# The last expert's rows reach the tokens by one-hot products, all other rows are gathered earlier; index keys loaded in pieces; a shorter routing

## What is computed

```python
def hier_moe(h, w_group, b_group, w_router, b_router, w_gate, w_up, w_down):
    ...
    g_w, g_idx = lax.top_k(jax.nn.softmax(g_logits, axis=-1), 1)
    ...
    e_in = e_logits[jnp.arange(m), g_idx[:, 0]]
    top_v, top_i = lax.top_k(e_in, TOP_K_INNER)
    top_w = jax.nn.softmax(top_v, axis=-1) * g_w
    ...
    for e in range(N_EXPERTS):
        hid = jax.nn.silu(x2 @ w_gate[e]) * (x2 @ w_up[e])
        y = y + combine[:, e:e + 1] * (hid @ w_down[e]).astype(jnp.float32)
```

## Time and profile before

| | |
|---|---|
| median of 3 runs | 1548.93 us (1548.56 to 1549.74) |
| profiled execution, its own time | 1553.47 us |
| its span | 1551.6 us |
| PE, DVE, ACT, POOL busy | 1360.3, 606.3, 305.6, 124.9 us |
| granted PE clock, mean | 0.928 |
| DMA | 341.04 MB, mean 220 GB/s |

### The profile page before, as it was taken

The page is one execution under the profiler, slowest core; times in us unless marked ns, Lnnn a source line. Parts: engine busy times, 40 slices in busy tenths (PEclk is TensorE's granted clock), DMA queues, the critical chain, the costliest instruction groups (busy, mean ns, idle before and its releaser), DMA issues.

```text
span 1551.6 us, 28263 instructions
## 1 busy us (share of the span) xinstructions
PE 1360.3 (88%) x10889; PEld 765.2 (49%) x10890; DVE 606.3 (39%) x1542; ACT 305.6 (20%) x777; POOL 124.9 (8%) x374
## 2 busy tenths in 40 slices
PE   7999998899689999998599987888999599998990
PEld 4454454454555555554543433455646365555550
DVE  2169733251513111110547997666303422111115
ACT  2121133321100000001303112455601000000102
POOL 1010190001000000000200000000000100000002
PEclk9999989899789999999599998899999699999995
DMA  8523567761658999998301021332443479999975
GB/s 266 200 52 119 187 200 229 226 264 41 249 196 323 360 391 398 399 402 341 128 5 55 31 109 55 110 108 73 131 175 120 156 304 344 394 387 388 396 289 194
DMA packets 87385, 341.04 MB, mean 220 GB/s; under 512 B 25671, under 2 KB 32935, under 8 KB 73286
## 3 DMA queue, kind: packets, MB, share of 16 engines
q1 hardware_dynamic: 67246, 289.40, 50.8%
q0 software_dynamic: 10656, 37.56, 7.1%
q10 hardware_dynamic: 9344, 12.20, 2.3%
HBM read 309.00 MB, written 30.47 MB: 219 GB/s over the span
## 4 chain that ended last, share of the span: by engine, by line
PE 63%; DVE 14%; DMA 12%; SPq 4%; issue 4%; ACT 2%; POOL 1%; POOLq 0%; ACTq 0%; DVEq 0%
PE banks L1161 19%; DMA arena<-in_wstream 9%; PE banks L840 9%; PE banks L1189 8%; PE banks L1067 6%; DVE arena L1746 4%; PE banks L868 3%; SPq L458 2%; PE banks L818 2%; PE banks L987 2%; DVE arena L1874 2%; DVE arena L1868 2%; PE banks L798 1%; DVE arena L1896 1%; DVE arena L1893 1%
## 5 line engine op out<-in xcount | busy, mean ns | idle before, releaser
L1161 PE MATMUL banks<-arena 128*32 128x128 f32 (+1 forms) x4736 | 363.3, 337 | 25.5 <-DMA arena<-in_wstream 13.1
L1161 PEld LDWEIGHTS banks<-arena 128*32 128x32 f32 (+1 forms) x4736 | 242.7, 127 | 145.3 <-issue 52.7
L1189 PE MATMUL banks<-arena 128*64 128x512 f32 (+1 forms) x1184 | 173.3, 492 | 1.1 <-ACT arena L1641 1.1
L1746 DVE TENSOR_TENSOR arena<-arena,banks 128x256 f32<-128x256 f32 (+5 forms) x84 | 38.5, 459 | 278.5 <-PE banks L1161 181.2
L840 PE MATMUL banks<-arena 128*128 128x512 f32 x320 | 144.0, 605 | 0.5 <-DMA arena<-in_wstream 0.5
L2118 DVE COPY arena<-banks 128x256 f32<-128x256 f32 (+1 forms) x56 | 21.4, 382 | 295.6 <-PE banks L1174 289.3
L1746 DVE TENSOR_TENSOR arena<-banks,arena 128x512 f32<-128x512 f32 (+5 forms) x159 | 70.7, 474 | 137.0 <-ACT arena L1565 81.3
L1067 PE MATMUL banks<-arena 128*128 128x512 f32 x256 | 115.4, 609 | 3.6 <-ACT arena L1681 2.3
L868 PE MATMUL banks<-arena 128*128 128x512 f32 x256 | 118.1, 606 | 0.0
L1641 ACT ACTIVATE arena<-banks 128x512 f32<-128x512 f32 (+1 forms) x56 | 29.6, 529 | 369.3 <-PE banks L1189 369.3
L1189 PEld LDWEIGHTS banks<-arena 128*64 128x64 f32 (+1 forms) x1184 | 59.6, 123 | 83.7 <-issue 68.3
(11 more groups left out here) (278 smaller groups left out, 1419.0 us busy)
## 6 DMA issues: line engine op xcount, KB each, us to landing
arena<-in_wstream SPq DMA_DIRECT2D x109, 2048.0 KB, 13.2
arena<-in_fox_kt SPq DMA_DIRECT2D x64, 256.0 KB, 3.1
arena<-in_fox_v SPq DMA_DIRECT2D x64, 256.0 KB, 3.0
arena<-in_dsa_page SPq DMA_DIRECT2D x64, 256.0 KB, 3.1
expert_rows<-arena ACTq DMA_DIRECT2D x76, 128.0 KB, 9.1
expert_rows<-arena POOLq DMA_DIRECT2D x1, 6656.0 KB, 19.4
hn_scratch<-arena POOLq DMA_DIRECT2D x8, 512.0 KB, 2.9
expert_rows<-arena ACTq DMA_DIRECT2D x68, 32.0 KB, 8.2
```

What stands on the lines that cost most here:

```text
L1161: last = mm(bank(b, 0, 4 * n, n * j, n * j + n), x[:, c, :], w[:, c, 4 * n * j:4 * n * j + 4 * n], start=(c == 0), stop=(c == DC - 1))
L1189: last = mm(bank(3, 0, 8 * n, n * q, n * q + n), ht2[g % 2][:, 128 * i + n * j:128 * i + n * j + n], w[:, c, 8 * n * q:8 * n * q + 8 * n], ...
L1746: return v.tensor_tensor(out, x, y, op)
```

## The change

Three edits. **(1)** The down product of the last group of slot 14 (g = 25) moves ahead of the up product of g = 26. POOL waits only for the stores of groups 0 to 25 and issues the ten gathers of the combine then (`combine` before `spilled`); a token whose row belongs to the last expert reads a row of zeros (ZROW, 128 rows more are zeroed at the start). The two groups of the last expert are not stored: they stay in SBUF (`y2`, `y_last`), and PE makes for each tile a product of a one-hot matrix `match` (which token each row belongs to, built by DVE at g = 10 and 11) with them (`last_expert`). DVE adds first all ten gathered pieces (`landed_rows`), then for each tile the product with the weight `w_last` (`combine_tile`). The row arithmetic of DVE is spread over g = 7 to 11. **(2)** The 64 key loads are cut into pieces of 12, 12, 26, 8 and 6 between the weight blocks. **(3)** In `route`, two steps become one, one loses its wait, a pair of memsets becomes one earlier memset, and a subtraction moves behind `mask`.

```diff
+SAVED = ENDS[NE - 2]
+ZROW = NROWS + SPILLS * CAP
...
-        for s in range(NS):
-            for j in range(NPG):
+
+        def index_keys(n0, n1):
+            for n in range(n0, n1):
+                s, j = divmod(n, NPG)
...
             if l == 0:
+                index_keys(0, 12)
                 sp.wait_ge(S("ln_done"), 1)
                 first_weights(0, 1, 0)
+                index_keys(12, 24)
             sp.wait_ge(S(f"out_mm{l}"), upto(f"out_mm{l}", 5))
             first_weights(l, 0, 1)
+            if l == 0:
+                index_keys(24, 50)
             sp.wait_ge(S(f"out_mm{l}"), upto(f"out_mm{l}", 10))
             first_weights(l, 0, 2)
+            if l == 0:
+                index_keys(50, 58)
             sp.wait_ge(S(f"route_mm{l}"), upto(f"route_mm{l}", 1))
             first_weights(l, 1, 2)
+            if l == 0:
+                index_keys(58, NS * NPG)
...
         def combine(l):
 
-            pool.wait_ge(S(f"row_u{l}"), upto(f"row_u{l}", 1))
+            pool.wait_ge(S(f"row_u{l}"), upto(f"row_u{l}", 2))
+            pool.wait_ge(S("zeros_out"), 16)
+            pool.wait_ge(S(f"xg_used{l}"), upto(f"xg_used{l}", NE))
+            pool.wait_ge(S(f"up_mm{l}"), upto(f"up_mm{l}", SAVED))
             for i in range(4):
-                pool.wait_ge(S(f"y_rows{l}_{i}"), upto(f"y_rows{l}_{i}", max(STORED[i::4])))
+                pool.wait_ge(S(f"y_rows{l}_{i}"), upto(f"y_rows{l}_{i}", max(STORED[i:SAVED:4])))
             for t in range(NT):
                 for k in range(2):
                     i = 2 * t + k
+                    if i == 7:
+                        pool.wait_ge(S(f"gate_mm{l}"), upto(f"gate_mm{l}", GROUPS))
...
+                if g == SAVED:
+                    down(g - 1)
...
-                if g > 0:
+                if g == GROUPS - 1:
+                    down(g - 1, lambda: turn_hid(g))
+                elif g > 0 and g != SAVED:
                     down(g - 1)
-            turn_hid(GROUPS - 1)
             down(GROUPS - 1)
+
+        def last_expert(l):
+
+            def share(t, i, y, n):
+                b = (4, 6, 0, 2, 0)[t]
+                for k in range(2):
+                    last = mm(bank(b + k, 0, 512, 0, rows(t)), match[i][64 * k:64 * k + n, 128 * t:128 * t + rows(t)],
+                              y[64 * k:64 * k + n, :], start=(i == 0), stop=(i == 1))
+                if i == 1:
+                    last.then_inc(S(f"down_mm{l}"), 1)
...
+            for t in range(2, NT):
+                if t == 4:
+                    pe.wait_ge(S(f"combined{l}"), upto(f"combined{l}", 3))
+                share(t, 0, y2[(GROUPS - 2) % 4], 64)
+                share(t, 1, y_last, 32)
...
+            v.memset(ghot[64:128, 4, :], 0.0).then_inc(S("dve_chain"), 1)
+            dve.wait_ge(S("dve_chain"), chained())
...
-            v.tensor_scalar(g3(sm[6], NT), hots[0], NEG, None, ALU.mult).then_inc(S("dve_chain"), 1)
+            v.scalar_tensor_tensor(out=e_in, in0=hots[0], scalar=NEG, in1=e_in, op0=ALU.mult, op1=ALU.add)\
+                .then_inc(S("dve_chain"), 1)
             dve.wait_ge(S("dve_chain"), chained())
-            tt(e_in, e_in, g3(sm[6], NT), ALU.add).then_inc(S("dve_chain"), 1)
-            dve.wait_ge(S("dve_chain"), chained())
...
+        def landed_rows(l):
+
+            for t in range(NT):
+                if t > 0:
+                    dve.wait_ge(S(f"yb{l}_{t}"), upto(f"yb{l}_{t}", 32))
+                for k in range(2):
...
+                    step(weighted(t, k))
...
         def combine(l):
             n = 2 * l + 2
-            for t in range(NT + 2):
+            dve.wait_ge(S(f"turns{l}"), upto(f"turns{l}", 1))
+            flag = spill_flag(dve)
+            landed_rows(l)
+            spilled(l, flag)
+            for t in range(NT + 3):
                 if t < NT:
                     combine_tile(l, t)
                 if 1 <= t <= NT:
                     mean_square(n, t - 1)
-                if t >= 2 and l == 0:
-                    to_xt(n, t - 2)
+                if t >= 3 and l == 0:
+                    to_xt(n, t - 3)
```

More of the change, by code:

```diff
@@ L396, in further_rounds @@
                         body(i)
+            if at_end:
+                at_end()
     def page_rows(ap, page):
@@ L1176, in turn_hid, with down @@
                 last.then_inc(S(f"ht_mm{l}"), 1)
-            def down(g):
+            def down(g, between=None):
                 s, off, n = PARTS[g]
@@ new lines, in _, with late_rows @@
+        row_of, over = g3(rtmp[0], NT), g3(rtmp[3], NT)
+        def late_rows(l):
+            some = g3(rtmp[1], NT)
+            step(tt(over, pos, bc_mid(cap_e, NT), ALU.is_ge))
+            step(tt(row_of, over, bc_mid(delta, NT), ALU.mult))
+            step(tt(row_of, row_of, pos, ALU.add))
+            step(v.scalar_tensor_tensor(out=row_of, in0=row_of, scalar=-float(ZROW), in1=bc_mid(base_e, NT),
+                                        op0=ALU.add, op1=ALU.add))
+            step(tt(some, row_of, over, ALU.mult))
+            per_choice(some, sm[3], float(ZROW))
+            v.tensor_copy(row_late, sm[3][:, 0:2 * NT])
@@ L2097, in xgt_evac, with last_matches @@
+        def last_matches(l):
+            for i in range(2):
+                for t in range(NT):
+                    last = v.tensor_scalar(match[i][:, 128 * t:128 * t + rows(t)], slot16[:, 0:rows(t)], 128.0 * t,
+                                           slot_tok[i], ALU.add, ALU.is_equal)
+            last.then_inc(S(f"row_u{l}"), 1)
         def xgt_evac(l, par, banks, n, done):
@@ L2155, in turn, with late_rows @@
                 tt(hid, g3(sil, 4), g3(bank(1), 4), ALU.mult).then_inc(S(f"general{l}_"), 1)
-            dve.wait_ge(S(f"turns{l}"), upto(f"turns{l}", 1))
-            further_rounds(dve, turn)
+            def late_rows():
+                dve.wait_ge(S(f"late{l}_"), 16 * 2 * NT)
+                for k in range(2):
+                    for t in range(NT):
+                        last = weighted(t, k)
+                    last.then_inc(S(f"late_sum{l}_"), 1)
+                    dve.wait_ge(S(f"late_sum{l}_"), k + 1)
@@ new lines, in spilled, with weighted @@
+            further_rounds(dve, turn, at_end=late_rows, flag=flag)
+        def weighted(t, k):
+            hv = h[0:rows(t), t, :]
+            return v.scalar_tensor_tensor(out=hv, in0=ybuf[2 * t + k][0:rows(t), :],
+                                          scalar=wts[0:rows(t), NT * k + t:NT * k + t + 1], in1=hv,
+                                          op0=ALU.mult, op1=ALU.add)
+        def landed_rows(l):
+            for t in range(NT):
+                if t > 0:
+                    dve.wait_ge(S(f"yb{l}_{t}"), upto(f"yb{l}_{t}", 32))
+                for k in range(2):
+                    if t == 0 and k == 0:
+                        dve.wait_ge(S("yb_first"), 16 * l + 16)
+                    if t == 0 and k == 1:
+                        dve.wait_ge(S(f"yb{l}_0"), upto(f"yb{l}_0", 16))
+                    step(weighted(t, k))
```

176 lines of the change are left out of this document (110 added, 66 removed).

## The result

The forecast was 1542.3 us, range 1538.2 to 1546.5. The medians differ by 10.5 us the other way.

The account below looks back on a forecast made before the run. The chain was read as 63% PE, with gains sought in three stretches where PE stands still. Terms -3.1 - 0.7 + 1.5 - 4.3 = -6.6 us took the median 1548.93 to 1542.3 us, range 1538.2 to 1546.5.

Parts of the forecast that it names:

- Front, -3.1 and -0.7: Layer 0's first expert gather, 7.3 us, falls to layer 1's 4.2 through cut key loads (-3.1); shorter routing in both layers, -0.7.
- Where the gathers start: Combine gathers start 7.3 us earlier in layer 0, 12.5 in layer 1, after the turn (transpose of g = 25).
- T: End of the ten sums of gathered pieces on DVE, forecast at 750.7 us in layer 0 and 1530.0 in layer 1.
- The one-hot products wait for nothing of this ... at about 0.27 us each: 16 of PE's 20 last-expert products run beside gathers and sums, done by 737 us (layer 0) and 1523 (layer 1).
- Layer 0 from T: First tile transpose at T+7.2, clock up 12 us later, wide projection at T+25.3: a loss of 1.5 us.
- Layer 1, -4.3: Five bank sums and five final norms take 13.9 us from T, ending at 1543.9 against 1548.2: -4.3 us.
- Sum: Both layers' terms together: -3.1 - 0.7 + 1.5 - 4.3 = -6.6 us.
- POOL held up by DVE: Rival: DVE's sums make each of 20 combine gathers cost 1 us more; +13 in total, 1562 us; chance 0.08.
- The early stores: Rival: layer 0's stores land in 1.6 us instead of 6.8, making its term -1.7; 1539.1 us; chance 0.17.
- 0.52: Chance of the forecast's own case, whose terms with smaller uncertainties reach from 1540 to 1544.8 us.
- half of 0.23: Two rivals near the 1545.8 bound: cut key loads do nothing (1545.4, chance 0.13); layer 0's restart worse (1544.8, chance 0.10).

Follow-up runs that it names:

- undisturbed trace: The changed kernel without the further rounds' code on all engines, on the first of two chips: ratio 0.9986 (0.9966 to 1.0006), turn to end 44.1 us.
- Seven beside the weight stream: The kernel before with seven added, unread gathers from hn_scratch near layer 1's last products, on two chips: ratios 0.9986 and 1.0010.

## Why the prediction was wrong, point by point

- **Front, -3.1 and -0.7: right in the rows** (first gather 7.27 to 4.13). Measured alone, -2.8 us of 3.8, with an interval from about -5.7 to 0.
- **Where the gathers start.** Layer 1 right (7.0 us behind the turn). Layer 0 wrong: I carried the 6.8 us landing over from stores one group later; at the new place, in the thick of the weight stream, the last took 11.6. T came 42.0 us behind the turn instead of 36.2, 4.8 of the 5.8 by the gathers' start. The new order costs 7.8 us from the first gather to the wide projection (48.3 against 40.5; 9.5 to 10.0 in the three other traces), where the forecast has 8.8; what is missing is above all the head start.
- **"The one-hot products wait for nothing of this ... at about 0.27 us each": wrong in price and place.** One fp32 product stands in the trace as two records (the program's 20 have 40), so the "four" of the earlier trace rows were two products of 0.56 us. In layer 1 the twenty took 11.5 us at a mean granted clock of 0.86 and 19.3 at 0.50, where I had 5.4. And they began 4.6 us (layer 1) and 6.1 us (layer 0) behind the copy that frees them, for the jump over the rounds' code. In layer 0 the fifth tile's took 3.87 and not 1.8.
- **Layer 0 from T.** The wide projection came at T+23.4 instead of T+25.3, although the first transpose was later (T+9.3 instead of T+7.2): the granted clock was 0.61 from 757 to 759 us and 1.00 behind that, at T+13, where I had T+19.2. In sum +5.3 us in the first trace where I had +1.5. From turn to wide projection it is 65.3, 67.0, 67.3 and 67.0 in the four traces of the changed kernel, 57.5 to 60.4 in seven traces with the old combine.
- **Layer 1, -4.3: this is the step that failed.** The sum lets ten gathers run beside PE's last products for nothing; no term and no rival prices what they do to PE. They put off the end of its last product by 13.2 to 14.5 us in all four traces of the changed kernel (29.8 us behind the turn in the first, 16.1 before). The ten sums stand behind that product's copy, so T came 39.5 to 40.7 us behind the turn where I had 29.4; in two of the four a second thing came on top, for which the sum has no term either: after the jump the products ran at half clock, and from T to the end it was 21.0 us where I had 13.9 (14.1 and 14.5 in the other two). Turn to end 61.0, 54.3, 60.5, 55.2: +6.7 to +13.4 where I had -4.3. The undisturbed trace (44.1, -3.5) shows that the rest of the term, 22.4 us of gathers and sums and 13.9 of tiles, was nearly sound: T 30.7 behind the turn, the tiles 13.5.
- **Sum.** -2.8, +5.3 and +13.4 make +15.9 for the profiled executions; their difference is 7.3. The turn of layer 0 came 10.5 us sooner in the trace after, of which the forecast gives the front 3.5; but in the traces without edits 2 and 3 it stands anywhere from 701.9 to 714.5 us, so the rest is scatter of the stages ahead. The second trace of the changed kernel gives -2.8 + 7.0 + 6.7 = +10.9, beside 10.5 for the medians.
- **Without the hold-up** the forecast would not have come true either. In the undisturbed trace layer 0 takes 64.5 us from turn to wide projection, so -2.8 + 4.5 - 3.5 = -1.8 us, as its ratio of 0.9986 says, and not -6.6.
- **The rivals.** POOL held up by DVE did not come: 909 to 1494 ns a gather. The early stores did not come, but their opposite. The outcome, slower by 0.76%, had 0.07 in the forecast, all of it on a mechanism that did not occur. (By its own rule the chance of "faster" was 0.52 + 0.17 + half of 0.23 = 0.805, not 0.79.)

What stays open is why PE stops. Shown: gathers on POOL's software queue, running at full DMA share beside products, hold up PE's results on four chips of the five that are named in the record; on the fifth they do so in neither of two programs, both of which were held up on another chip. It does not take their source, their target, or the kernel's other parts. Not every product is stopped: in layer 0 of the first trace the 32 records of one-hot products above (727.94, 9.77 us) stand without a break beside the gathers, at a DMA share of 1.04; nothing waits for their results just then, so whether these were late can't be seen. Not tried: as many bytes by a hardware queue at the late moment, with no weight stream beside; so whether the queue or the moment is at fault isn't told apart. Nor was the unaltered kernel run on the fifth chip. The version with edits 2 and 3 alone has 0.998, the interval just reaching 1; it is faster than the changed kernel, and not clearly faster than the one before.

## What to carry to other kernels

A transfer moved beside an engine's work is not free because the queue was idle there: look for an engine that gets results late ("remote" in its idle time, though the producer's records ended long ago), and measure the overlap by itself, in the old kernel, at the very moment planned. When a merge step is changed from "each tile when its pieces are there" to "all pieces first", the head start must be worth more than the lost overlap; here the new order cost 7.5 to 8.4 us from the first gather to the end of layer 1 in the two traces without hold-up. Take a product's price from the number of products that the program makes, not from the number of records (two for each fp32 product here), and price a landing at the place to which the store is moved.

## What the runs showed of the hardware

- Ten gathers of 128 rows x 4 KB on POOL's queue, at a DMA share of 0.84 to 1.03, made PE's results come 5 to 14 us late, on four chips; single products then came about 0.72 us apart. Seven beside the weight stream: 3.8 us in one trace, 0 in another. One chip of five showed none of it in two programs.
- The jump over the rounds' code on PE: the next product starts 4.3 to 7.5 us behind the copy that frees it, 0.10 us without that code. In nine traces with the jump the granted clock fell while PE stood idle, and 32 records took 9.5 to 15.5 us; in four without it stayed at 1.00 (8.14 us).
- Four 32 KB stores issued in 1.75 us landed after 7.0 to 11.6 us beside the weight stream, after 1.6 us without.
- An fp32 product stands in the trace as two records: 40 for the 20 of `last_expert`.
